# Attention with the denominators summed from row scores on ScalarE and folded into the key scores of one hybrid trunk layer

## What is computed

```python
def one_block(qblk):
    s = jnp.einsum("bkgqd,bkld->bkgql", qblk, k).astype(jnp.float32) * scale
    p = jax.nn.softmax(s, axis=-1).astype(v.dtype)
    return jnp.einsum("bkgql,bkld->bkgqd", p, v)
```

## Time and profile before

| | |
|---|---|
| median of 3 runs | 1472.0 us (1471.87 to 1472.65) |
| the profiled execution, its own time | 1468.41 us |
| its span | 1466.6 us |
| busy TensorE, VectorE, ScalarE, POOL | 1334.4, 730.4, 529.9, 41.8 us |
| granted clock of TensorE, mean | 0.955 |
| shares of the chain that ended last | PE 81%, DVE 8%, DMA 4%, ACT 3% |

### The profile page before, as it was taken

How to read it: one execution, slowest core, us unless ns; L and a number is a source line. 1 busy time by engine, 2 the same in 40 slices (tenths; PEclk the granted TensorE clock), 3 DMA queues, 4 the chain that set the end, 5 groups by cost and what they waited for, 6 DMA issues and landing times.

```text
span 1466.6 us, 31772 instructions
## 1 busy us (share of the span) xinstructions
PE 1334.4 (91%) x13955; PEld 1225.7 (84%) x13955; DVE 730.4 (50%) x1085; ACT 529.9 (36%) x796; POOL 41.8 (3%) x84
## 2 busy tenths in 40 slices
PE   5799998997999799959993989979999999989996
PEld 2699997997998455559982968879999999989995
DVE  3517743722544479955445542164554545433534
ACT  3635534421233444312333212173333434333433
POOL 0000010000000000000001000000000000000000
PEclk8899999999999799989996999999999999999998
DMA  9222263314000200020006467311212121012222
GB/s 395 76 89 101 97 265 133 130 46 168 8 4 3 87 0 0 1 95 8 4 3 241 148 238 283 114 58 58 86 57 86 60 83 65 15 57 72 71 72 93
DMA packets 24761, 134.58 MB, mean 92 GB/s; under 512 B 2992, under 2 KB 3632, under 8 KB 16208
## 3 DMA queue, kind: packets, MB, share of 16 engines
q1 hardware_dynamic: 19088, 103.59, 19.9%
q0 software_dynamic: 5568, 29.40, 5.3%
HBM read 112.66 MB, written 20.32 MB: 91 GB/s over the span
## 4 chain that ended last, share of the span: by engine, by line
PE 81%; DVE 8%; DMA 4%; ACT 3%; issue 1%; PEld 1%; POOL 0%; POOLq 0%; PEldq 0%; SPq 0%; DVEq 0%; ACTq 0%
PE ps L675 43%; PE ps L1120 10%; PE ps L838 4%; PE ps L826 3%; PE ps L806 2%; PE ps L1025 2%; PE ps L710 1%; PE ps L984 1%; PE ps L818 1%; DMA xT<-in_x 1%; DVE rden L1801 1%; PE ps L700 1%; PE ps L1002 1%; PE ps L949 1%; DMA attention_scratch<-attention_inputs_made 1%
## 5 line engine op out<-in xcount | busy, mean ns | idle before, releaser
L675 PE MATMUL ps<-h2lo,whi 128*128 128x322 f32 x672 | 154.5, 311 | 0.7 <-ACT facc L1220 0.7
L675 PE MATMUL ps<-h2hi,wlo 128*128 128x322 f32 x672 | 155.0, 312 | 0.0
L675 PE MATMUL ps<-h2hi,whi 128*128 128x322 f32 x672 | 154.0, 310 | 0.0
L1511 DVE TENSOR_TENSOR wlo<-raw,whi 128x2048 fp32r<-128x2048 f32 x48 | 109.7, 2287 | 76.3 <-ACT whi L1182 76.3
L675 PE MATMUL ps<-hlo,whi 128*128 128x322 f32 x544 | 128.3, 317 | 1.0 <-ACT qkv L1246 1.0
L675 PE MATMUL ps<-hhi,wlo 128*128 128x322 f32 x544 | 125.7, 312 | 0.0
L675 PE MATMUL ps<-hhi,whi 128*128 128x322 f32 x544 | 125.0, 311 | 0.0
L675 PEld LDWEIGHTS ps<-h2hi,whi 128*128 128x128 f32 x672 | 114.2, 190 | 0.0
L675 PEld LDWEIGHTS ps<-h2lo,whi 128*128 128x128 f32 x672 | 113.0, 189 | 0.9 <-DVE wlo L1511 0.9
L675 PEld LDWEIGHTS ps<-h2hi,wlo 128*128 128x128 f32 x672 | 113.7, 189 | 0.0
L1555 DVE SCALAR_TENSOR_TENSOR facc<-fraw,par,facc 128x642 f32<-128x642 f32 x44 | 39.0, 887 | 139.2 <-ACT facc L1220 139.2
(11 more groups left out here) (312 smaller groups left out, 2643.8 us busy)
## 6 DMA issues: line engine op xcount, KB each, us to landing
raw<-in_wblk SPq DMA_DIRECT2D x48, 1024.0 KB, 4.8
adl<-in_wada SPq DMA_DIRECT2D x8, 2048.0 KB, 8.2
raw<-in_wdn SPq DMA_DIRECT2D x44, 256.0 KB, 2.6
adaw<-in_wada SPq DMA_DIRECT2D x4, 2048.0 KB, 17.6
gate_scratch<-gout POOLq DMA_DIRECT2D x16, 322.0 KB, 2.7
gld<-gate_scratch POOLq DMA_DIRECT2D x8, 644.0 KB, 4.1
attention_inputs_used<-attention_scratch SPq DMA_DIRECT2D x1, 5056.0 KB, 14.6
u_scratch<-uout POOLq DMA_DIRECT2D x12, 320.0 KB, 2.4
```

The source lines that it names most:

```text
L675: mm = pe.matmul(o, w, v, start=first, stop=last and w is hi and x is xh[n])
L1511: TT(wlo[s][:, :], raw[s][:, :], whi[s][:, :].bitcast(F32), ALU.subtract).then_inc(lo_done, 1)
```

## The change

The attention is reordered: all 32 row-score units of the latent queries come first, then all key scores and values.

- The context rows come ahead of everything. The row scores use three buffers in turn. ScalarE takes the exponential of each unit in place, with the negative maximum as its bias, and sums it by row into den (`row_exponentials`). The logarithm of den, taken in two halves, and the maximum give one column for each head and query tile, negative maximum less the logarithm (`lse_columns`), split into a rounded part and the rest. TensorE turns these columns into rows (`lse_turn`), and VectorE multiplies them with a mask for each head into partitions 64 to 127 of a second copy of the queries, q2 (`lse_row`); partitions 0 to 63 of q2 are loaded by SyncE. The lower half of the second part of k is now 1.0.
- So `key_scores(u, c)` has two matmuls for each head, and its second one also adds the row; there is no third one, and its exponentials are already divided by the denominator. For the same reason the second matmul of a row score uses 64 rows only.
- `values(u, c)` makes two matmuls, one for each head of the pair, with 64 columns of V as weights and without the ones, into the two halves of the output partitions. VectorE copies the output of a pair of heads (`heads_out`), without reciprocals. The context keeps its diagonals and its reciprocals.
- The products of the preparation stand between steps by `head_ticks`. The one at i = 4 waits for the context's output (o_copied).
- In the gates stage the preparation moves by two tiles, on TensorE, ScalarE and VectorE (on VectorE `4 <= t < 12` instead of `2 <= t < 10`). POOL's wait for the stores of the gates moves from ahead of the second barrier to ahead of the third.

```diff
--- before.py
+++ after.py
@@ -265,11 +267,15 @@
     assert spot[0] <= norm_end
     spot[0] = ring_at
     pt = [sb(f"pt{s}", [P, 6, LAT]) for s in range(2)]
-    mdiag = [sb(f"mdiag{s}", [P, 4, P], F32R) for s in range(2)]
-    cdiag = [sb(f"cdiag{s}", [P, 4, P]) for s in range(2)]
+    cdiag = [pt[s][:, 4, :].rearrange("p (t n) -> p t n", t=4) for s in range(2)]
+    rden = pt[1][:, 3, :]
+    aT = sb("aT", [P, 4, TP])
     nmax = sb("nmax", [P, 40])
-    rden = [sb(f"rden{s}", [P, LAT]) for s in range(2)]
-    aT = sb("aT", [P, 4, TP])
+    den, lnd, nlse = (sb(name, [P, 32]) for name in ("den", "log_den", "neg_lse"))
+    lse_hi = sb("lse_hi", [P, 32], F32R)
+    lse_cols = sb("lse_columns", [P, 4, 64])
+    q2f = [sb(f"q_and_lse{s}", [P, 4, LAT]) for s in range(2)]
+    q2 = [q[:, :, :].bitcast(F32R) for q in q2f]
...
+                sp.wait_ge(barrier, 12)
+                for s in range(2):
+                    sp.wait_ge(rw_st[s], 16)
+                for p in range(2):
+                    sp.dma_start(q2f[p][0:64], qa_s[0:64, 3072 + 2048 * p:5120 + 2048 * p].rearrange("p (j n) -> p j n", j=4))\
+                        .then_inc(q2_ld, 16)
...
-        for s in range(2):
-            gp.wait_ge(g_st[s], 16 * NBLK_G)
         phase_over(gp, 2)
...
         presets(0)
+        for s in range(2):
+            gp.wait_ge(g_st[s], 16 * NBLK_G)
         phase_over(gp, 3)
-        gp.wait_ge(o_copied, 10)
+        gp.wait_ge(o_copied, 5)
...
-            if t == 1:
+            if t == 3:
                 for s in range(2):
                     prepare_product(0, s)
-            elif t % 2 == 0 and 2 <= t < 10:
+            elif t % 2 == 0 and 4 <= t < 12:
                 for j in range(2):
-                    prepare_product(0, t + j)
+                    prepare_product(0, t - 2 + j)
...
             if 2 <= i < 4:
                 prepare_product(1, i - 2)
             elif 0 <= e < 4 and k in (0, 2):
+                if i == 4:
+                    pe.wait_ge(o_copied, 1)
                 prepare_product(1, 2 + 2 * e + k // 2)
...
         def row_scores(n):
 
-            h, qt = n // 4, n % 4
-            pe.wait_ge(max_done, n)
-            q = qst_u[h % 2][:, h // 2, qt * P:qt * P + P]
+            u, h, qt = n // 8, n // 4, n % 4
+            unit = n + 1 if n < 20 else n + 2
+            if n == 22:
+                pe.wait_ge(lse_rows, 4)
+            elif unit == 3:
+                pe.wait_ge(max_done, 1)
+            elif unit > 3:
+                pe.wait_ge(rexp_done, n - 2 if n < 20 or n > 22 else n - 1)
+            at = row_buffer(unit)
+            q = qst_u[h % 2][:, u, qt * P:qt * P + P]
             for a, w in ((0, 512), (512, 256)):
-                for part in range(2):
-                    mm = pe.matmul(psf[:, a:a + w], q, kst_u[:, part, h // 4, a:a + w], start=part == 0, stop=part == 1)
+                out = psf[:, at + a:at + a + w]
+                pe.matmul(out, q, kst_u[:, 0, u // 2, a:a + w], start=True, stop=False)
+                mm = pe.matmul(out, q[0:64], kst_u[0:64, 1, u // 2, a:a + w], start=False, stop=True)
             mm.then_inc(row_s_done, 1)
 
+        def lse_turn(half, b):
+
+            pe.wait_ge(lse_done, half + 1)
+            for qt in range(4):
+                mm = pe.matmul(bank(b, P, P * qt)[64:128], lse_cols[:, qt, :], ident, start=True, stop=True)
+            mm.then_inc(lse_turned, 1)
...
         def context_rows():
-            pe.wait_ge(max_done, 32)
             for j in range(4):
...
-        def key_scores(h, c):
-
-            m = 6 * h + c
-            if m >= 2:
-                pe.wait_ge(exp_done, m - 1)
-            out = bank(2 + m % 2)
-            for part in range(2):
-                pe.matmul(out, kst_u[:, part, h // 4, c * P:c * P + P], qst_u[h % 2][:, h // 2, :], start=part == 0, stop=False)
+        def key_scores(u, c):
+
+            for p in range(2):
+                m = 12 * u + 2 * c + p
+                if m < 4:
+                    pe.wait_ge(rexp_done, 30 if m < 2 else 32)
+                else:
+                    pe.wait_ge(exp_done, m - 1)
+                if c == 0:
+                    pe.wait_ge(lse_rows, 2 * u + p + 1)
+                out = bank((m + 2) % 4)
+                pe.matmul(out, kst_u[:, 0, u // 2, c * P:c * P + P], qst_u[p][:, u, :], start=True, stop=False)
+                pe.matmul(out, kst_u[:, 1, u // 2, c * P:c * P + P], q2[p][:, u, :], start=False, stop=True)\
+                    .then_inc(st_done, 1)
+
+        def context_scores():
+            for p in range(2):
+                pe.wait_ge(diag_done, 1 + p)
+                pe.matmul(bank(6 + p), onesr[:, :].bitcast(F32), cdiag[p].rearrange("p t n -> p (t n)"), start=True, stop=False)
+                rows = slice(64 * p, 64 * p + 64)
+                for j in range(4):
+                    mm = pe.matmul(bank(6 + p, P, P * j), k2c_u[rows, j // 2, :], qc[rows, j, :], start=False, stop=j == 3)
+                mm.then_inc(st_done, 1)
+
+        def values(u, c):
+
...
-                    pe.wait_ge(o_copied, h - 1)
-            pe.wait_ge(exp_done, 6 * h + c + 1)
-            at = 64 - 64 * (h % 2)
-            mm = pe.matmul(bank(4 + h % 2), vo_u[:, c, h // 4, at:at + P], pt[h % 2][:, c, :], start=c == 0, stop=c == 5)
...
-        for qt in range(4):
-            row_scores(qt)
-        for h in range(8):
-            nxt = [lambda n=n: row_scores(n) for n in range(4 * h + 4, 4 * h + 8)] if h < 7 else [context_rows] + [lambda: None] * 3
-            key_scores(h, 0)
-            nxt[0]()
-            between_heads(4 * h + 0)
-            key_scores(h, 1)
-            values(h, 0)
-            key_scores(h, 2)
-            nxt[1]()
-            between_heads(4 * h + 1)
-            values(h, 1)
-            key_scores(h, 3)
-            nxt[2]()
-            between_heads(4 * h + 2)
-            values(h, 2)
-            key_scores(h, 4)
-            nxt[3]()
-            between_heads(4 * h + 3)
-            values(h, 3)
-            key_scores(h, 5)
-            values(h, 4)
-            if h == 7:
-                context_scores(0)
-            values(h, 5)
...
-        for p in range(2):
-            context_values(p)
+                if u == 0:
+                    pe.wait_ge(rexp_done, 31)
+                elif u == 1:
+                    pe.wait_ge(lse_rows, 8)
+                else:
+                    pe.wait_ge(o_copied, u)
+            pe.wait_ge(exp_done, 2 + 12 * u + 2 * c + 2)
+            for p in range(2):
+                mm = pe.matmul(bank(4 + u % 2)[64 * p:64 * p + 64], vo_u[:, c, u // 2, 64:128], pt[p][:, c, :], start=c == 0,
+                               stop=c == 5)
+            mm.then_inc(pv_done, 1)
+
+        def context_values():
+
+            pe.wait_ge(exp_done, 2)
+            pe.wait_ge(prep_read, 14)
+            for b, a in ((6, 64), (7, 0)):
+                for g in range(2):
+                    for p in range(2):
+                        mm = pe.matmul(bank(b, 256, 256 * g)[64 * p:64 * p + 64], vo_u[:, 6, g, a:a + 64],
+                                       pt[p][:, 5, 256 * g:256 * g + 256], start=True, stop=True)
+            mm.then_inc(pv_done, 1)
+
+        context_rows()
+        for n in range(32):
+            row_scores(n)
+            if n == 3:
+                context_scores()
+            if n == 13:
+                pe.wait_ge(exp_done, 2)
+                between_heads(2)
+            if n == 18:
+                between_heads(3)
+            if n == 19:
+                pe.wait_ge(rexp_done, 18)
+                lse_turn(0, 0)
+            if n == 23:
+                context_values()
+        pe.wait_ge(q2_ld, 32)
+        for u in range(4):
+            for c in range(6):
+                key_scores(u, c)
+                if u == 0 and c == 5:
+                    pe.wait_ge(rexp_done, 31)
+                    lse_turn(1, 5)
+                for i in head_ticks(u, c):
+                    between_heads(i)
+                if c >= 2:
+                    values(u, c - 2)
+            values(u, 4)
+            values(u, 5)
         phase_over(pe, 4)
...
                 if t == 0:
                     low_tanh()
+                elif t == 2:
                     key_squares(0)
-                elif t == 1:
+                elif t == 3:
                     for s in range(2):
                         key_norm_log(0, s)
                     for s in range(2):
                         key_norm(0, s)
...
+        def row_exponentials(n):
+
+            unit = n + 1 if n < 20 else n + 2
+            out = psf[:, 1024 * (unit % 3):1024 * (unit % 3) + 768]
+            ac.wait_ge(max_done, n + 2)
+            ac.activation(out, out, ACT.Exp, bias=nmax[:, n:n + 1], accum_out=den[:, n:n + 1]).then_inc(rexp_done, 1)
+
+        def denominator_logs(half):
+            ac.wait_ge(rexp_done, 16 * half + 16)
```

(45 more changed lines are left out.)

157 lines of the change are left out of this document (74 added, 83 removed).

## The result

The change makes the kernel slower. Median of 6 runs 1483.85 us (1480.53 to 1489.35) against 1471.93 us before (6 runs, 1469.04 to 1472.74): ratio 1.0088, 95% interval 1.0067 to 1.0109, so about 12 us. The forecast was 1455 us, 17 less. The profiled execution took 1483.22 us, its span is 1481.4 us.

The account below looks back on a forecast made before the run. TensorE was taken to bound the kernel. Attention -8.6, gates -7.3 and POOL's drain -2.0 gave 17.9 us less; 0.9 was left for small waits, so 1472.0 - 17.0 = 1455 us, range 1436 to 1487.

Parts of the forecast that it names:

- Gates: Gates stage: later key products no longer wait for the uc load, -7.3 us; POOL's drain before the barrier begins earlier, -2.0.
- Crossing, key scores and values: Attention after the row scores: 4.3 us wait at the crossing, 61.7 for 24 key-score and value steps, 0.8 last copy.
- a restart: Attention stage: half clock expected behind each of two long TensorE stalls, 1.9 us each, 3.8 together.
- the wait for the context's output: Crossing to key scores: first preparation product waits for last maximum, four reciprocals and a multiplication, 4.3 us.
- The third rival: Key scores and values: value pairs run one after another, +21 us, 1476 us; chance 0.07.
- Prices in the row part: Row part: units 1.45 us each, 46.4 for 32; other TensorE work 10.8; waits 8.1.
- The second rival: Attention: height switches are free, ScalarE sets the row part at 1.1 us a unit, 1436 us; chance 0.12.
- The stall for exponential 16: Row part: TensorE waits for ScalarE's table loads, logarithms and exponentials ahead of row exponential 16, 4.3 us.
- The wait for the lse rows: Row part: unit 22 waits for four 64x512 VectorE multiplications behind maximum 20, 2.3 us.
- The 1.5 us behind units 5 and 9: Row part: context exponentials and squares on ScalarE hold buffers, costing 0.55 + 0.95 us over the slack.
- The clock: Row part: half clock for only some 5 us at the start, 1.4 us, since TensorE no longer waits at once.
- my first rival: Row part: TensorE at half clock, units say 2.5 us, 1487 us; chance 0.22 throughout, 0.12 in part.

Follow-up runs that it names:

- the run with the low part of the keys: Changed kernel, all row-score matmuls 128 rows, low part of keys held there during row scores, POOL writing the ones afterwards: 1443.50 us, ratio 0.9815 to the kernel before.
- 128 rows throughout: Changed kernel with the second and fourth matmul of each row score back at 128 rows: 1443.56 us, ratio 0.9812 to the kernel before.
- the units all of 64 rows: Changed kernel with all four matmuls of each row score at 64 rows: 1453.68 us, ratio 0.9884 to the kernel before.
- the run with one switch a unit: Changed kernel, row-score matmuls grouped by height, every second unit in the other order: 1453.04 us, ratio 0.9874 to the kernel before.
- the one with two: Changed kernel, each row score doing its two 128-row matmuls first, then its two 64-row ones: 1464.14 us, ratio 0.9952 to the kernel before.

## Why the prediction was wrong

**Gates: right.** Forecast -9.3; the chunks start 8.9 us earlier, and alone the part is worth 11. The wait for uc is gone from the view of waits. One piece went otherwise than forecast: POOL's drain began with the last tile (331.94 us) and lasted 4.18 us, not 3.34, so 0.8 us of what the store had cost came back in the drain. What I did not have is the first chunk stage, 1.5 us longer; its cause stays open (the clock is 0.66 between 353 and 358 us, which I did not take further).

**Crossing, key scores and values: right in sum.** Forecast 4.3 + 61.7 + 0.8 and 1.9 for a restart, 68.7 us; from 577.77 to 647.34 us it is 69.6. Two of its terms miss in opposite ways, and that much is luck: the wait for the context's output is 3.07 us and not 4.3, and TensorE works at half clock for some 8 us around it, up to 589 us, which costs about 4 us (half of that work) and not 1.9. Value pairs do run beside each other: four matmuls of 512 columns in 1.01 us (590.37 to 591.38), where one after another they would take 4 x 0.43 = 1.72. A steady step takes 2.12 us (590.37 to 592.49), forecast 1.78 + 0.36 = 2.14. The third rival is dead.

**Prices in the row part: right.** A switch was to cost 0.19 us at 2.4 GHz: the unit is 1.48 us at full clock against 1.45 forecast, and 0.70 without switches. The second rival, free switches, is dead. The row exponential was to take 0.90 + 0 to 0.2: it takes 874 + 193 ns, and the two overlap, since such pairs start 0.88 us apart in the run with the low part of the keys. The stall for exponential 16 was to be 4.3: 4.35. The wait for the lse rows was to be 2.3 and is 1.39 here, since the slow unit 21 hides more of it; with 128 rows throughout it is 2.61. The 1.5 us behind units 5 and 9 do not appear here.

**The clock: this step failed.** The sum had "plus 1.4 us for a start at half clock of some 5 us, less than before since TensorE no longer waits at once". The row part then took 98.1 us in place of 66.7 and 1.9 for a restart, 29.5 us too much; that is as much as the whole miss of 29 us. Its parts: the 32 units, 72.5 us and not 46.4, +26.1; the other TensorE work, 19.8 and not 10.8, +9.0; shorter waits, 5.7 and not 8.1, -2.4; and the 1.4 + 1.9 = 3.3 us that the forecast had already put down for half clock. The premise behind the 1.4 us was that a TensorE without gaps gets its clock back. The trace shows otherwise: 48.00 of 48.00 us busy at 0.50 here, 9.13 of 12 us busy at 1.00 in the run with 128 rows throughout. The Trainium skill ("TensorE: Matmul & The Clock Gate", HAM oscillation) ties the low clock to waits between bursts of matmuls. The falls of the 128-row run, each with a wait before it, agree with that; the falls of the changed kernel at 531 and 568.6 us, with no wait, do not, so it is not the whole rule.

I had the right case as my first rival, with the right unit (2.5 us; 2.47 measured) and the right place, 1487 us against 1483.85, and gave it 0.22. "Against it: here it has work all the time" was what tipped it, a reason that the earlier trace rows could not carry: there the gaps came together with full-height units, so that view could not tell gaps from height. The rival's own words, that a unit streams for 0.64 of 1.45 us and drains for the rest, were the better reading, and still not the whole: the units all of 64 rows, with no switch inside them, were held at half clock too.

What stays open: how much of the effect in the four-switch unit belongs to the drain time and how much to the empty rows. The pair of 128 and 64 rows shows that rows alone suffice; the run with one switch a unit leaves the low clock after some 30 us while the one with two does not up to 536 us, with the same columns and rows, which suggests that switches matter as well. It does not show it: there is one profile of each, and the changed kernel with its four switches rose behind the same preparation product, for some 4 us. I have no run with full rows and drains.

## What to carry to other kernels

Before a matmul is cut to half its rows, ask what stands beside it: among full matmuls the cut cost some 0.2 us a switch and left the clock alone, in a stretch of its own it can take the clock of everything there. A half that holds zeros, or old data that the sum can bear, cost no time here (0.70 us a unit at 2.4 GHz), and with it the clock was high in most of the row part; let an idle engine write the right values there later. And a busy TensorE at a low granted clock is a reason to look at the heights of its matmuls in the groups by shape, not only for waits.

## What the runs showed of the hardware

- With units that alternate 128 and 64 rows, TensorE stayed at 1.2 GHz while busy without a gap (48.00 of 48.00 us at 0.50), and fell back to it without one (568.6 us). With units all of 64 rows it was held there even without switches inside them (9.91 of 10.00 us busy at 0.50).
- The same kind of unit can run at either level in one execution: with four needless full matmuls ahead of the four of a row score, 2.41 us a unit in the 38 us at 1.00 and 4.18 us a unit behind the stall, with TensorE busy 14.00 of 14.00 us at 0.50.
- With units of 128 rows it had 2.4 GHz with short gaps (9.13 of 12.00 us busy at 1.00), and lost it for a while with waits of 1.35, 4.35 and 2.61 us. Zeros in the upper 64 rows made no difference that shows in the time (1446.16 against 1443.50 us).
- A switch between 128 and 64 rows costs 0.20 us at 2.4 GHz ((1.48 - 0.70) / 4) and 0.30 at 1.2 GHz ((2.47 - 1.28) / 4). Among full matmuls it was 0.17 at 2.4 GHz ((1.38 - 0.69) / 4).
- Summing by row in an activation adds an instruction of 193 ns behind the 874 ns of 768 columns; the two overlap, and in the run with the low part of the keys two such pairs start 0.88 us apart:

```profile
496.09 0.89 ACT L1445 ACTIVATE ps<-ps,nmax 128x768 f32<-128x768 f32 x1
496.87 0.23 ACT L1445 ACTIVATION_READ_ACCUMULATOR ps<-ps,nmax 128x1 f32 x1
496.97 0.90 ACT L1445 ACTIVATE ps<-ps,nmax 128x768 f32<-128x768 f32 x1
```

- Two matmuls of 512 columns that write different halves of the output partitions run side by side: four in 1.01 us.
